# Layer 2's key scores from a product of query weights and keys, six of its sixteen parts made during the scan and parked in memory

## The reference, cut to what matters

```python
q = (hb @ w_q).reshape(PEER_BLOCK, PEER_HEADS, 2, PEER_DHALF)      # 8 heads x 2 x 256
s = jnp.einsum("nhkd,hkmd->nhkm", q, sub_keys)                      # 128 keys each
s_half, i_half = lax.top_k(s, PEER_TOPK)                            # 16 of 128
cand = s_half[:, :, 0, :, None] + s_half[:, :, 1, None, :]
top_s, top_c = lax.top_k(cand.reshape(..., 256), PEER_TOPK)
```

## Time and profile before

| | us |
|---|---|
| median of the three timed runs (3845.73, 3846.15, 3854.15) | 3846.15 |
| the profiled execution, its own time | 3855.96 |
| its span in the trace | 3854.2 |
| the scan: PE's dummies begin, the readout begins | 2806.9, 2855.5 |
| output projection ends | 2924.2 |
| key scores on PE | 2929.9 to 3056.2 |
| building of the gates | 3077.5 to 3167.3 |
| experts of layer 2 | from 3169.8 |

### The profile page before, as it was taken

The page is one execution under the profiler, slowest core; times in us unless marked ns, Lnnn a source line. Parts: engine busy times, 40 slices in busy tenths (PEclk is TensorE's granted clock), DMA queues, the critical chain, the costliest instruction groups (busy, mean ns, idle before and its releaser), DMA issues.

```text
span 3854.2 us, 61506 instructions
## 1 busy us (share of the span) xinstructions
PE 3751.7 (97%) x21356; PEld 3172.9 (82%) x21356; DVE 2966.6 (77%) x5358; ACT 1590.8 (41%) x2440; POOL 115.9 (3%) x153
## 2 busy tenths in 40 slices
PE   8999999999999999999999999999989999999998
PEld 7897799556988888888888888888768888888887
DVE  7533275896898899999887899998566997777776
ACT  6301052232137444444484444444332194444443
POOL 0000000000000000000000000000400000000000
PEclk9999999999999999999999999999999999999999
DMA  5314464475422655555515777777735415555554
GB/s 197 104 50 151 145 202 151 162 227 188 164 90 83 204 193 193 197 191 192 188 56 196 239 237 236 239 239 238 171 122 178 161 63 197 189 191 190 191 190 153
DMA packets 204274, 669.52 MB, mean 174 GB/s; under 512 B 36000, under 2 KB 46288, under 8 KB 202592
## 3 DMA queue, kind: packets, MB, share of 16 engines
q1 hardware_dynamic: 159936, 577.31, 45.3%
q0 software_dynamic: 19872, 80.86, 6.8%
q10 hardware_dynamic: 24320, 9.37, 0.9%
HBM read 639.21 MB, written 27.21 MB: 173 GB/s over the span
## 4 chain that ended last, share of the span: by engine, by line
PE 88%; DVE 9%; ACT 1%; DMA 1%; issue 1%; SPq 0%; DVEq 0%; ACTq 0%; POOLq 0%
PE psum L1116 27%; PE psum L1102 16%; PE psum L1104 9%; PE psum L736 5%; PE psum L1195 5%; PE psum L761 4%; PE psum L676 4%; PE psum L1290 3%; PE psum L1081 2%; PE psum L1386 2%; PE psum L1184 2%; DVE arena L2462 1%; DVE arena L2463 1%; PE psum L1161 1%; DVE arena L2464 1%; PE psum L1488 1%
## 5 line engine op out<-in xcount | busy, mean ns | idle before, releaser
L1116 PE MATMUL psum<-v_split,coef_split 128*128 128x512 f32 x4284 | 1034.1, 390 | 0.0
L1102 PE MATMUL psum<-input_split,u_split 128*128 128x512 f32 x2800 | 987.0, 391 | 0.0
L1116 PEld LDWEIGHTS psum<-v_split,coef_split 128*128 128x128 f32 x4284 | 779.7, 188 | 157.1 <-issue 1.2
L1104 PE MATMUL psum<-input_split,u_split 128*128 128x256 f32 x2800 | 788.9, 282 | 0.0
L1102 PEld LDWEIGHTS psum<-input_split,u_split 128*128 128x128 f32 x2800 | 525.3, 188 | 112.7
L1104 PEld LDWEIGHTS psum<-input_split,u_split 128*128 128x128 f32 x2800 | 528.5, 189 | 16.2
L1794 ACT ACTIVATE work<-work 128x256 f32<-128x256 f32 x350 | 146.7, 419 | 851.2 <-DVE work L2604 851.2
L1577 ACT ACTIVATE v_split<-ring 128x1024 fp32r<-128x1024 f32 x357 | 379.7, 1063 | 234.8 <-PE psum L1116 229.0
L2599 DVE TENSOR_TENSOR u_split<-ring,u_split 128x1024 fp32r<-128x1024 f32 x377 | 459.7, 1219 | 12.4 <-ACT u_split L1577 12.4
L2604 DVE TENSOR_REDUCE work<-psum 128x256 f32<-128x512 f32 x350 | 242.1, 692 | 258.8 <-PE psum L1104 257.5
L2599 DVE TENSOR_TENSOR v_split<-ring,v_split 128x1024 fp32r<-128x1024 f32 x357 | 433.9, 1216 | 2.3 <-ACT v_split L1577 2.3
(11 more groups left out here) (466 smaller groups left out, 4722.9 us busy)
## 6 DMA issues: line engine op xcount, KB each, us to landing
ring<-in_u SPq DMA_DIRECT2D x384, 512.0 KB, 3.3
ring<-in_v SPq DMA_DIRECT2D x384, 512.0 KB, 3.3
ring<-in_w SPq DMA_DIRECT2D x324, 512.0 KB, 3.4
arena<-in_ada POOLq DMA_DIRECT2D x48, 512.0 KB, 4.4
scratch_inj<-stage ACTq DMA_DIRECT2D x16, 512.0 KB, 5.2
arena<-scratch_inj POOLq DMA_DIRECT2D x7, 1024.0 KB, 7.8
scratch_cm<-work POOLq DMA_DIRECT2D x8, 512.0 KB, 6.4
scratch_cm<-arena POOLq DMA_DIRECT2D x8, 512.0 KB, 4.9
```

The costliest lines, as they stand in the source:

```text
L1102: mm(bank(b), rows[:, 0, P * k:P * k + P], HR[:, k, :, :], start=(k == 0), stop=False, skip_group_check=True)
L1104: last = mm(bank(b)[:, 0:S], rows[:, 1, P * k:P * k + P], HR[:, k, 0, :], start=False, stop=(k == 7), skip_group_check=True)
L1116: last = mm(bank(2 + 2 * i + f), CFR[:, b, c, P * i:P * i + P], parts[:, v, 512 * f:512 * f + 512], start=(first and c == 0 and v == 0), s ...
```

## The change

Layer 2's scores are made in the second way too, as layer 1's.

- The 16 parts of W·K need 32 slots: 12 (`wk_scan`, parts 0 to 5, heads 0 to 2) stand in the stream between `ssm_in` and `ssm_out`, 20 (`wk_last`) where `q1` was.
- During the scan PE makes parts 0 to 5 in place of 44 dummies, and 16 dummies stay behind them. ACT copies each part's high half to one buffer, PE subtracts it from PSUM (a product with minus the identity matrix, `less_high`), and ACT copies what is left, the low half, to another. ACT's DMA queue writes both to memory and loads the keys, a 128 KB block for each part. All of it stands ahead of `states` in ACT's program.
- POOL, behind the last batch of the readout, loads the whole key table, the parked parts of head 0, and once DVE has begun the last normalisation those of heads 1 and 2; its parking of X stands behind these.
- In `peer_last` PE makes parts 6 and 7 ahead of the input, then for each head the scores with 48 fp32r matmuls, subtractions for the head two further on and the parts of the head three further on. ACT copies high and low halves (`last_keys`); `queries` is gone. There are three buffer pairs instead of two.
- 64 instead of 44 of the tiles ahead's matmuls come before the choice ends, fewer between the builds, and ACT's gelu of tiles 4 to 9 comes six steps earlier.
- Some semaphores are renamed or shared; this changes no wait.

```diff
+NSCAN = 6
-                  ("wq", 32), ("ssm_in", 8), ("ssm_out", 16), ("q1", 40)):
+                  ("wq", 32), ("ssm_in", 8), ("wk_scan", 2 * NSCAN), ("ssm_out", 16),
+                  ("wk_last", 32 - 2 * NSCAN)):
...
 # POOL
+            def heads_back(h):
+                for kk in range(2):
+                    for part in range(2):
+                        pool.dma_start((LASTL if part else LASTH)[h][:, :, P * kk:P * kk + P].bitcast(F32),
+                                       io["wk"][2 * h + kk, part].rearrange("p (k m) -> p k m", k=KD_))\
+                            .then_inc(sem("wk_back"), 16)
+                pool.wait_ge(sem("wk_back"), 64 * h + 64)
+            pool.wait_ge(sem("high_parked"), 16 * NSCAN)
+            pool.wait_ge(sem("low_parked"), 16 * NSCAN)
+            pool.wait_ge(sem("y_summed"), 2)
+            pool.dma_start(KT.rearrange("p n d m -> p (n d m)"), io["keys2"]).then_inc(sem("tables_loaded"), 16)
+            heads_back(0)
+            pool.wait_ge(sem("inputs_scaled"), 5 * KD_ + 1)
+            heads_back(1)
+            heads_back(2)
...
 # PE
+            def unit(n, keys, off):
+                for d in range(2):
+                    arrived(L.slots)
+                    for t in range(8):
+                        last = mm(PS(off + P * t, P), ring[:, L.slots % RING, P * t:P * t + P], keys[:, d, :],
+                                  start=(d == 0 and t % 4 == 0), stop=(d == 1), skip_group_check=True)
...
+                L.mark(last, "scores_made")
+            def less_high(n, high, off):
+                pe.wait_ge(sem("wk_copied"), 2 * NH + n + 1)
+                for f in range(2):
+                    last = mm(bank(off // 512 + f), MINUS, high[f], start=False, stop=True, skip_group_check=True)
+                L.mark(last, "scores_made")
...
-            keep_busy(44, 4)
+            for n in range(NSCAN):
+                if n >= 2:
+                    pe.wait_ge(sem("wk_low"), 2 * NH + n - 1)
+                pe.wait_ge(sem(f"keys_loaded{n % 2}"), 16 * (n // 2) + 16)
+                unit(n, SCANK[n % 2], 2048 + 1024 * (n % 2))
+                if n:
+                    less_high(n - 1, (WKHO[:, 0:512], WKHO[:, 512:1024]), 2048 + 1024 * ((n - 1) % 2))
+            less_high(NSCAN - 1, (WKHO[:, 0:512], WKHO[:, 512:1024]), 2048 + 1024 * ((NSCAN - 1) % 2))
+            pe.wait_ge(sem("wk_low"), 2 * NH + NSCAN - 1)
+            keep_busy(16, 4)
...
+                pe.wait_ge(sem("tables_loaded"), 128)
+                evacuated()
+                made(3)
+                keep_busy(3, 6)
+                L.take("input_parts")
+                for h in range(NH):
+                    last_scores(h)
+                    if 1 <= h <= 5:
+                        less(h + 2)
+                    if 1 <= h <= 4:
+                        made(h + 3)
                 beside = up_ahead(2)
-                fill(beside, 32)
+                fill(beside, 64)
                 for _ in range(2):
                     L.take("key_scores_used")
-                fill(beside, 12)
                 turn_choice(KK)
                 fill(beside, 9)
                 L.take("chosen_evacuated")
                 for n in range(32):
                     build(64 + n, n % 2, n < 2)
-                    fill(beside, 1 if n % 3 == 2 else 2 if n < 31 else 8)
+                    fill(beside, 2 if n % 4 == 3 else 1)
...
 # ACT
+            def scan_unit(n):
+                o = 2048 + 1024 * (n % 2)
+                act.wait_ge(sem("scores_made"), 3 * NH + (2 * n if n else 1))
+                if n:
+                    act.wait_ge(sem("high_parked"), 16 * n)
+                copy(WKHO, PS(o, D)).then_inc(sem("wk_copied"), 1)
+                act.wait_ge(sem("wk_copied"), 2 * NH + n + 1)
+                act.dma_start(io["wk"][n, 0], OUTS[0]).then_inc(sem("high_parked"), 16)
+                if n + 2 < NSCAN:
+                    scan_keys(n + 2)
+                act.wait_ge(sem("scores_made"), 3 * NH + min(2 * n + 3, 2 * NSCAN))
+                if n:
+                    act.wait_ge(sem("low_parked"), 16 * n)
+                copy(WKLO, PS(o, D)).then_inc(sem("wk_low"), 1)
+                act.wait_ge(sem("wk_low"), 2 * NH + n + 1)
+                act.dma_start(io["wk"][n, 1], OUTS[1]).then_inc(sem("low_parked"), 16)
...
+            for n in range(NSCAN):
+                scan_unit(n)
             states(slice(0, 16))
             L.give(states(slice(16, NG)), "scanned")
...
-                    queries()
+                    L.taken["scores_made"] = 3 * NH + 2 * NSCAN
+                    for h in range(NSCAN // 2, NH):
+                        last_keys(h)
...
-                    if p == 2 and n in (8, 18):
-                        gelu_ahead(p, 4 if n == 8 else 8)
+                    if p == 2 and n in (2, 12):
+                        gelu_ahead(p, 4 if n == 2 else 8)
...
 # DVE
+            ts(MINUS, ident, -1.0, None, ALU.mult)
```

152 lines of the change are left out of this document (76 added, 76 removed).

## The result

The changed kernel takes 3867.1 us (median of five, 3866.82 to 3872.58) against 3849.88 for the kernel before (median of five, 3845.73 to 3854.15): ratio 1.0046, 95% interval 1.0034 to 1.0057. It is slower by 17 us, more than the 11.5 us that count as a difference, and outside the forecast range. The place is the one that the prediction named for its second rival: the parking becomes the bound of the scan, with the state copies behind it on ACT.

A forecast was written before the change was run, and what follows sets the result against it. PE, busy 97% of the span, was taken as the bound, with DVE a close second in the key scores. -9.8 + 7.1 - 1.9 + 0.5 = -4.1 us gave 3851.9 against the profiled execution, 3842 against the median; range 3834 to 3856.

The forecast's parts named there:

- rival 2: Scan: ACT's wait to write the single high buffer becomes the bound; P = 9.9, loss 22.1 us, 3857; chance 0.12.
- The choice: Layer 2's key scores: DVE sets the pace at 15.1 us a choice and starts 7.0 us earlier; gain 9.8 us.
- The scan: Six parts made and parked during the scan delay ACT's last state copy from 2855.4 to 2862.5; loss 7.1 us.
- P: Period of one part in the scan, from PE, copies, landing and bytes; taken as 6.9 us.
- the term of 7.1 us: Loss in the scan from ACT's state copies ending later, at P = 6.9.
- 2828.0 + 5P: Scan: when ACT's last state copy ends, behind six parts; 2862.5 at P = 6.9.
- Rival 1: The scan covers all the added work: P 5.4 to 5.9, loss 0 to 2 us, 3836; chance 0.25.
- Rival 3: TensorE falls to half its clock in the scan: P = 9.3, loss 19.1 us, 3854; chance 0.07.
- The readout: Behind the scan: dummies run up to the readout, so it no longer starts at 1.2 GHz; gain 1.9 us.
- The projection: Output projection: key table and head 0, 4 MB, meet its weights; bounds 0 and 3 us, 0.5 taken.
- The stretch behind the choice: From the eighth choice on: unchanged; 20 fewer matmuls ahead in the building costed at 0, as ACT covers it.

The follow-up runs named there:

- The kernel without slots: Changed kernel with no slots loaded for the scan's six parts, made from the output projection's two slots; all writes stay: 3859.02 us, ratio 1.0018.
- one part written: Changed kernel, but only the last of the scan's six parts is written to memory, two writes instead of twelve: 3855.24 us, ratio 1.0007.
- the kernel with the keys first: Changed kernel with ACT issuing the next key block's load ahead of the high half's copy and write, not behind the write: 3867.15 us, ratio 1.0044.

## Why the prediction was wrong, step by step

**The choice** (-9.8 forecast, -9.4 measured) was right in size and in mechanism: first choice 6.7 us nearer to the split, DVE setting the pace at 15.14 us with no wait, PE done long before.

**The scan** is the step that failed, "I take P = 6.9". The place was named (rival 2: the parking becomes the bound, state copies behind it on ACT), the term of 7.1 us was mis-sized and measured 18.9. P was worked out for a part alone: 2.23 MB, and the landing of 5.2 us from layer 1's writes. The sentence that the first parts must share with POOL's batches stood there without a price. The sum that was missing adds up all bytes of the stage first: six parts make 13.4 MB, POOL's batches and the like another 6.4, together the 19.8 MB that the trace counts. At the 300 GB/s that this very place showed before that is 66 us, at 348 it is 57, and ACT's state copies, 10.2 us, still stand behind them. Either is longer than the 48.6 us that the scan had to give. Four parts make 15.3 MB, 44 us at 348 GB/s: they fit, as measured. Such a sum warns, but it is a floor and not the time. The kernel without slots moved 13.5 MB, 39 us at 348 GB/s, and its state copies ended at 58.5 us and not at 49, for ACT's waits for single landings stay.

The runs bear it out: fewer writes or fewer reads shorten the part to 6.8 or 6.9 us on average, the same bytes without the wait leave it at 8.3, and two or four parts cost the scan no time at all. Rival 2 had put all of it on the wait for the high buffer; the runs show that wait and the bytes, neither of them small.

By the measured P of 8.89 the prediction's own formula, 2828.0 + 5P, gives 2872.5 for the last state copy, and it ended at 2871.9. That it comes so near is in part luck. PE began 2.0 us earlier than taken, and the tail behind the sixth high copy took 17.0 us, not 15.8. The formula lets the sixth low copy trail by 4.2 us, for a next part that the sixth doesn't have: without waits it trails by 1.8 (one part written), and here by 5.4, for the landing.

Rival 1 had a chance of 0.25 on the same mistake. Rival 2 had 0.12; its "against" rested on layer 1's landing of 5.2 us, and in the scan a high half took 7.4. A sum in it is off as well: the loss reaches 11.2 us at P = 7.7, not 7.9, where it is 12.1. And by the choice's own terms the eighth choice comes at 3048.4, not 3048.6. Neither matters for the forecast.

The rate was not what failed. The Trainium skill (DMA: Bandwidth & Descriptors, Specifications) gives about 358 GB/s as what HBM gives one core. Over the 38 us with the engines always busy the trace shows 348, a little below it; the kernel with the keys first shows 371 over 38 us, above it. Put to a part's bytes it makes P 6.2, further off than the 6.9 taken; put to the stage's 19.8 MB it makes 55 us (an estimate from the page's figure), ahead of the state copies.

**Rival 3**, half the clock, happened in pieces that don't carry the loss. The granted clock was 0.87 in 2804 to 2842: 0.74 in 2806 to 2812, 0.62 in 2818 to 2824, where PE was busy 2.1 of 6 us, and 1.00 from 2830 to 2848. The matmuls of the first three parts took about 3.6 us longer for it, where 1.7 had been taken.

**The readout** (-1.9, measured -1.8) was the right number with half of its reason, and that is luck. The clock was full, as said, but part of the gain is that POOL's batches had landed in the longer scan. With nothing parked and the scan at before's length, full clock went with 13.3 and 13.6 us, a lower one with 13.9 to 14.5: 0.3 to 1.2 us, and none in the time. With two parts parked the readout took 14.8 us at full clock.

**The projection** (+0.5, measured +4.4): the upper bound of 3 us was too low. ACT waited 5.53, 1.77 and 1.75 us for slots, PE stood 2.67 us behind the first of these waits, and it was granted 0.86 over 2900 to 2912, where before it had 1.00 (2883 to 2895). The experiment that moves the 4 MB away gives 53.7 again. With the key table alone it took 54.3, 54.3 and 54.6 us in three traces and 59.7 in one.

**The stretch behind the choice** (0, measured +2.4) was missing altogether. I costed 20 fewer matmuls in the building at nothing because ACT covers them. They did more than fill: with one behind the last build instead of seven, PE idles 3.15 us before the experts, which then begin at a clock of 0.57 and take 1.4 us longer. The other 0.9 us lie at the turning of the chosen keys. PE's matmuls ahead now end earlier, it stands 6.06 us (0.40 before), and the turning runs at half the clock (granted 0.50 over 4 us, 1.00 before). Six dummies there and seven matmuls at the end gave both back in the trace; the time can't tell so little.

## What to carry to other kernels

Before work is put "under" a wait, add up the bytes that all queues will move in that stretch, those that are there already first, and divide by the rate that the stretch itself has shown. That gives a floor; waits for single landings come on top, and a landing time from another place says nothing of a stretch with other traffic. Such cover has an edge: up to it work is free in that stage (four parts), beyond it the stage grows (six), and the data still have to be loaded back beside something else. So size the work to the cover, or see whether it need be early at all, since here none of the sixteen parts had to be. And a count that fits one schedule (64 matmuls ahead, 42 dummies) is to be worked out anew when what stands before it moves.

## What was not expected of the hardware

- TensorE was granted 0.60 in the first 4 us of the readout behind 2.8 us without work, nearly as little as behind 8.8 us (0.51 to 0.67 in three traces), and 0.57 behind 3.15 us ahead of the experts; but gaps of 1.1 us, one before the readout and one every 5.4 us where a single part is written (2827 to 2842), left it at 1.00.
- Reads slow writes and the other way round at this load: the 512 KB write of a high half landed in 7.4 us beside slot loads, batches and keys, and in 5.1 with no slots loaded; a slot took 7.6 us in the scan, 4.9 where one part is written, and 3.4 in the projection.
- The same instructions' scan took 67.5, 67.7 and 71.7 us in three executions of kernels that do not differ there, where before's took 48.5 to 48.6 in every trace with dummies alone. Here the stage that hung on landings was also the one that scattered.
